# Moving weight units and activation buffers to other start addresses in SBUF, one core

## The reference

```python
# first block
proj  = rmsnorm(x, g_mix) @ w_in                  # 1024 -> 4804, attention inputs and gates
x     = x + merged_attention(proj, mem) @ w_out
hid   = square(relu(rmsnorm(x, g_mlp) @ w_mlp_in))  # 1024 -> 4096
x     = x + hid @ w_mlp_out
# second block: four of these (f = 0..3), with a gated mixer after f = 0
# and an attention after f = 2
def swiglu(x, w1, w3, w2):                        # 1024 -> 2816 -> 1024
    return (silu(x @ w1) * (x @ w3)) @ w2
h = layer_norm(ALPHA * h + 0.5 * swiglu(h, w1, w3, w2), g, b)
mix = (u * mixed) @ sgu_w_out                     # the gated mixer; u, v = split(gelu(h @ sgu_w_in))
```

## Time and profile before

| | |
|---|---|
| median of 3 runs | 1497.84 us (1495.8 to 1498.41) |
| the profiled execution's own time | 1496.87 us |
| its span, first to last instruction | 1495.1 us |
| TensorE busy | 1443.5 us, 97% of the span |
| VectorE busy | 930.3 us, 62% |
| ScalarE busy | 660.5 us, 44% |
| mean granted TensorE clock | 0.987 of full speed |
| HBM read | 261.92 MB, 178 GB/s over the span |

### The profile page before, as it was taken

The page is one execution under the profiler, slowest core; times in us unless marked ns, Lnnn a source line. Parts: engine busy times, 40 slices in busy tenths (PEclk is TensorE's granted clock), DMA queues, the critical chain, the costliest instruction groups (busy, mean ns, idle before and its releaser), DMA issues.

```text
span 1495.1 us, 25330 instructions
## 1 busy us (share of the span) xinstructions
PE 1443.5 (97%) x10484; PEld 1319.8 (88%) x10484; DVE 930.3 (62%) x1363; ACT 660.5 (44%) x834; POOL 95.7 (6%) x78
## 2 busy tenths in 40 slices
PE   8998998999999999999999999999999998999997
PEld 6987987899899999999789999999999886799996
DVE  5877457555675555657885555746555767665556
ACT  5655534333444434545244334425333467543342
POOL 0012141000020000100020000100000100100000
PEclk9999998999999999999999999999999999999999
DMA  7442444676577555655355555567555430465551
GB/s 256 151 141 88 153 142 155 218 222 215 189 235 272 193 186 188 198 193 197 113 186 201 186 191 197 192 202 253 188 184 193 157 135 24 141 205 191 195 196 57
DMA packets 191526, 268.43 MB, mean 180 GB/s; under 512 B 5740, under 2 KB 164752, under 8 KB 191182
## 3 DMA queue, kind: packets, MB, share of 16 engines
q1 hardware_dynamic: 186336, 250.05, 50.5%
q0 software_dynamic: 4224, 15.91, 3.1%
q10 hardware_dynamic: 878, 1.21, 0.3%
HBM read 261.92 MB, written 4.19 MB: 178 GB/s over the span
## 4 chain that ended last, share of the span: by engine, by line
PE 84%; DVE 9%; ACT 3%; DMA 2%; issue 1%; POOL 0%; DVEq 0%; ACTq 0%
PE bank L750 82%; DVE split L2009 2%; DMA ring<-in_ffn_w 2%; PE bank L773 1%; ACT split L1539 1%; DVE resid L2086 1%; DVE resid L2094 1%; DVE stats L2065 1%; DVE resid L2063 1%; ACT act_out L1561 0%; DVE arena L2601 0%; DVE stats L2023 0%; DVE arena L2206 0%; ACT gain_rows L1665 0%; DMA resid<-in_x 0%
## 5 line engine op out<-in xcount | busy, mean ns | idle before, releaser
L2009 DVE TENSOR_TENSOR split<-ring,split 128x2048 fp32r<-128x2048 f32 x212 | 484.4, 2286 | 371.2 <-ACT split L1539 365.8
L750 PE MATMUL bank<-hT_hi,split 128*128 128x256 f32 (+1 forms) x3984 | 699.9, 278 | 8.3 <-ACT act_out L1677 5.4
L750 PEld LDWEIGHTS bank<-hT_hi,split 128*128 128x128 f32 (+1 forms) x3984 | 609.2, 188 | 16.9 <-issue 9.8
L1539 ACT ACTIVATE split<-ring 128x2048 fp32r<-128x2048 f32 (+1 forms) x224 | 428.4, 1913 | 353.7 <-PE bank L750 318.2
L750 PE MATMUL bank<-hT_lo,split 128*128 128x256 f32 (+1 forms) x1992 | 552.4, 277 | 0.0
L750 PEld LDWEIGHTS bank<-hT_lo,split 128*128 128x128 f32 (+1 forms) x1992 | 375.3, 188 | 2.3
L750 PE MATMUL bank<-split,hid_hi 128*128 128x512 f32 x992 | 288.7, 397 | 0.0
L750 PEld LDWEIGHTS bank<-split,hid_hi 128*128 128x128 f32 x992 | 183.1, 189 | 39.1 <-issue 0.8
L750 PE MATMUL bank<-split,hT_hi 128*128 128x256 f32 (+1 forms) x896 | 178.0, 296 | 7.4 <-DVE split L2009 4.4
L750 PE MATMUL bank<-split,hid_lo 128*128 128x512 f32 x496 | 158.9, 393 | 0.0
L750 PEld LDWEIGHTS bank<-split,hT_hi 128*128 128x128 f32 x896 | 142.7, 189 | 15.8 <-issue 5.8
(11 more groups left out here) (216 smaller groups left out, 964.7 us busy)
## 6 DMA issues: line engine op xcount, KB each, us to landing
ring<-in_ffn_w SPq DMA_DIRECT2D x132, 1024.0 KB, 5.1
ring<-in_w_in SPq DMA_DIRECT2D x19, 1024.0 KB, 5.1
ring<-in_w_mlp_in SPq DMA_DIRECT2D x16, 1024.0 KB, 5.7
ring<-in_w_mlp_out SPq DMA_DIRECT2D x16, 1024.0 KB, 4.8
ring<-in_sgu_w_in SPq DMA_DIRECT2D x16, 1024.0 KB, 5.3
ring<-in_sgu_w_out SPq DMA_DIRECT2D x8, 1024.0 KB, 4.9
ring<-in_kv_w SPq DMA_DIRECT2D x6, 1024.0 KB, 5.2
ring<-in_w_out SPq DMA_DIRECT2D x4, 1024.0 KB, 5.0
```

The source lines that it names most:

```text
L750: ins = pe.matmul(o, lhsT, rhs, start=start, stop=stop)
L1539: act.activation(halves(q, n)[0], ring[:, u % SLOTS, 0:n], ACT.Copy).then_inc(hi_ready, 1)
L2009: dve.tensor_tensor(lo, ring[:, u % SLOTS, 0:n], hi.bitcast(F32), ALU.subtract).then_inc(split_ready, 1)
```

## The change

No instruction is added, removed or moved: each engine's list of instructions is the same before and after, row for row. Only start addresses differ. `LINE` becomes 512, so that a place is set modulo 512. The hi and lo halves of a `split` slot each get 128 spare elements, and a unit's start in its half depends on its kind.

Modulo 512 bytes the starts are now, with those of before in brackets:

- units that move token by token: 320 (192); the other units of the MLP, of FFNs 0 and 3, of the mixer, gates, `wout`, `q`, `wo`: 192 (192)
- units of the second FFN (f = 1) past its first chunk's `w1` and `w3`: 384 (192); units of the third (f = 2): 256 (192)
- `hid_hi`, `hid_lo`: 128 (320); `two`, `arena`: 128 (384); `const`: 128 (384); `hT_hi`, `hT_lo`, `ring`, `resid`, `xn`: 128 (128)

In the loops `halves` is asked for the unit one body later (`q + BODY`), since the first unit of the MLP's loop body moves token by token in its first turn and not in the later ones.

```diff
-LINE = 256
+LINE = 512
+SPARE = LINE // 4
+SHIFT = 32
...
+def by_token(name):
+
+    if name[0] in ("w1", "w3"):
+        return name[1] in TOK and name[2] == 0
+    return name[0] in ("proj", "sv") or name in (("mu", 0), ("mu", 1), ("kv", KV_ORDER[0]), ("kv", KV_ORDER[1]))
+
+
+def split_shift(q):
+
+    name = SPLIT_NAMES[q]
+    if by_token(name):
+        return SHIFT
+    if name[0] in ("w1", "w3", "w2"):
+        return {1: SHIFT + SHIFT // 2, 2: SHIFT // 2}.get(name[1], 0)
+    return 0
...
-        place(64)
+        place(128)
         with nc.sbuf_tensor("shared_rows", [P, 3 * MLP_BODY * 512], F32) as shared_rows:
...
         place(192)
-        split = sb("split", [P, SPLIT, 2, UNIT], F32R)
+        split = sb("split", [P, SPLIT, 2, UNIT + SPARE], F32R)
...
-            return [r[:, place, 0:n] for r in (split_hi, split_lo)]
+            at = split_shift(q)
+            return [split[:, place, part, at:at + n] for part in range(2)]
...
-                act.activation(halves(q, n)[0], ring[:, u % SLOTS, 0:n], ACT.Copy).then_inc(hi_ready, 1)
+                act.activation(halves(q if i is None else q + BODY, n)[0], ring[:, u % SLOTS, 0:n],
+                               ACT.Copy).then_inc(hi_ready, 1)
```

More of the change, by code:

```diff
@@ L208 @@
     n for n in plan_units() if n[0] != "cw")}
+SPLIT_NAMES = list(SPLITS)
 ORDER = plan_units()
@@ L380, in take @@
                                **{x: s for x, s in zip(names[:-1], shape[:-1])})
-        split_hi, split_lo = split[:, :, 0, :], split[:, :, 1, :]
         xn_flat = xn[:].rearrange("p b d -> p (b d)")
@@ L1072, in split_in_turn @@
                 pe.wait_ge(split_ready, i * BODY + (AHEAD + q + 1))
-                return [r.rearrange("p (k c) -> p k c", k=tiles) for r in halves(q, UNIT)]
+                return [r.rearrange("p (k c) -> p k c", k=tiles) for r in halves(q + BODY, UNIT)]
             def mlp(n):
@@ L2007, in low_unit @@
                 n = width(name)
-                hi, lo = halves(q, n)
+                hi, lo = halves(q if i is None else q + BODY, n)
                 dve.tensor_tensor(lo, ring[:, u % SLOTS, 0:n], hi.bitcast(F32), ALU.subtract).then_inc(split_ready, 1)
@@ L2660, in low_unit @@
             def low_unit(name):
-                q, u, place = SPLITS[name], UNITS[name], split_slot(SPLITS[name])
+                q, u = SPLITS[name], UNITS[name]
+                hi, lo = halves(q, UNIT)
                 pool.wait_ge(hi_ready, q + 1)
                 pool.wait_ge(split_ready, AHEAD + q)
-                pool.tensor_tensor(split_lo[:, place, :], ring[:, u % SLOTS, :], split_hi[:, place, :].bitcast(F32),
-                                   ALU.subtract).then_inc(split_ready, 1)
+                pool.tensor_tensor(lo, ring[:, u % SLOTS, :], hi.bitcast(F32), ALU.subtract).then_inc(split_ready, 1)
             pool.memset(zeros[:], 0.0)
```

## The result

The changed kernel takes 1507.41 us (median of 6, 1503.67 to 1511.03) against 1497.65 us; ratio 1.0065, 95% interval 1.0051 to 1.0079. The forecast was 1492.3, the range 1485 to 1503. The profiled execution took 1505.75 us.

The account below looks back on a forecast made before the run. TensorE's matmul pitch was taken to bound the kernel. Gains of 3.5 (tokens), 1.3, 0.6 and 0.3 (down units) less 0.2 (second memory unit) made 5.5 us, giving 1492.3 us; range 1485 to 1503.

Parts of the forecast that it names:

- What bounds the kernel: Whole kernel: TensorE, busy 97% of the span; outside seams, time is matmul count times pitch, so only pitch can move it.
- Features in FFNs 1 and 2: Feature matmuls with stationary starts 384 and 256 over moving 128: keep the fast 113.2 ns, nothing gained or lost.
- or 117.6: Upper bound in ns for the features of FFNs 1 and 2, the slow pitch already seen; would cost 8.9 us.
- rival 2: Features of FFNs 1 and 2 fall into the slow order, 8.9 us, time 1501.2; chance 0.22 with its wider form.
- Tokens: Token units at moving start 320 over stationary 128: 792 matmuls go from 117.6 to 113.2 ns, 3.5 us gained.
- Down units: Down matmuls: 1.3 us gained in MLP, mixer, FFNs 0 and 3; 0.6 in FFN 1; 0.3 in FFN 2.
- Features elsewhere: MLP, FFNs 0 and 3: own starts stay, only the down unit's hand-over may change; bounds nothing and 11.4 us, taken as nothing.
- The rule of the Trainium skill: TensorE has two independent SBUF read ports and never waits; taken to make the change worth nothing, the first rival, chance 0.26.

Follow-up runs that it names:

- experiment 5: Changed kernel with the starts of feature and down units set per FFN and MLP by a table in 64-byte steps; 1513.86 us, one run.
- experiment 7: experiment 1's kernel with hT, hid, two, arena and split all 64 bytes further; 1496.98 us, ratio 0.9985.
- experiment 9: Changed kernel with units of FFNs 1 and 2 moved by 256 bytes, to 448, in place of 192 and 64; 1497.58 us, ratio 0.9987.
- experiment 3: Kernel before, in the new split layout, with the token units alone moved by 128 bytes; 1498.29 us, ratio 1.0001.
- experiment 2: Kernel before, in the new split layout, with units of FFNs 1 and 2 alone moved, by 192 and 64 bytes; 1509.01 us, ratio 1.0070.
- experiment 4: Kernel before, in the new split layout, with hid, two, arena and const at 128 and no unit shifted; 1497.82 us, ratio 0.9988.
- experiment 11: experiment 1's kernel traced once more, unchanged; 1498.2 us, one run.
- experiment 12: The changed kernel traced once more, unchanged; 1507.6 us, one run.
- experiment 8: experiment 1's kernel with down units of the MLP and all four FFNs moving from 384; 1510.46 us, ratio 1.0080.
- experiment 1: Changed kernel with units of FFNs 1 and 2 put back to start 192, tokens at 320 and activations at 128 kept; 1496.39 us, ratio 0.9985.

## Why the prediction was wrong

**What bounds the kernel** was right: the 9 us are in the stages where TensorE hardly pauses, at a granted clock of 1.00, and there only pitches moved. The stage ahead of the MLP differs by up to 5 us between executions, with the change or without.

**The step that failed** is "Features in FFNs 1 and 2 ... I take 113.2: nothing", and with it the bound above it, "or 117.6". The two starts have pitches of their own, 119.9 and 118.6 to 118.7, above both pitches that the trace of before showed. They cost 6.2 and 5.0 us, 11.2 in all, where I had 0 with 8.9 as the worst. I had bounded an unseen pair of starts by the pitches of seen ones; experiments 5, 7 and 9 show that a pair is classed by its distance modulo 256, and no feature in the trace of before lay at the distances 0 and 128 of these two FFNs. This was rival 2, given 0.22, with the right place and too low a price.

**Tokens.** Right in kind and pitch (113.2). The mixer's gain is 1.5 us, and in all stages 2.5 (experiment 3) where I had 3.5; some short token stretches stay slow in each trace. 320 over 128 is distance 192, the features' own good one. What I had not seen is that features whose starts did not move are in the slow order behind them, in the mixer (+1.7) and `kv` (+0.8). Experiment 3 measured the whole of this step at 1.0001. In `kv` that goes with the tokens being fast, in all fourteen traces; in the mixer it came with the new layout even where the tokens stayed slow (experiments 2 and 4), so what it is owed to is not shown.

**Down units.** I took 231.2, 230.0 and 231.2 ns; the runs have 228.8, 227.9 and 232.3. The bounds, 229.0 to 233.3, held in the third and were just missed in the first; the second is lower still. The gain on TensorE is 3.6 ns x 1008 and 4.6 x 240, 4.7 us for my 1.9. But experiment 4, with all 62 units at 228.8 (5.4 us), came out at 0.9988, some 1.8 us. Its trace against that of before gives the reasons. The MLP and the four FFNs are 3.5 us shorter where their 55 down units alone would give 4.7: the features behind the faster units took 113.6 ns in place of 113.4, in the MLP 113.9 in place of 113.5, 0.9 us in all. And the features' slow order in the mixer and `kv` cost 2.5. FFNs that fall slow in some executions (about 4 us each, experiments 7, 11, 12) may come on top; how often they do was not measured.

**"Features elsewhere", taken as nothing,** is the second miss: mixer and `kv` lost 2.5 us of the 9. I had the mechanism, an order entered and then kept, and gave it a price only after down units. The sum of the first trace: 9.8 in FFNs 1 and 2 and 2.5 here, less 1.7 for tokens in the mixer and `kv` and 2.7 in the MLP and FFNs 0 and 3, is 8.0; the last 0.9 is the product's -0.7 and the queries' +1.7, which do not repeat.

**The rule of the Trainium skill** that I weighed against the trace (SBUF — State Buffer, "Who interferes with whom": TensorE's two read ports are independent and it never waits) does not hold here in the consequence that I drew from it, that a start address could not matter. The page itself says nothing of start addresses. With instructions, clock and other engines alike, a move of 192 bytes costs 6.5 ns on a 256-column matmul, and one of 256 bytes nothing. The runs show that the distance between the two streams matters; they do not show where in the memory or the engine the two meet.

## What to carry to other kernels

When a kernel is bound by back-to-back float32 matmuls, read the pitch of each kind of product from start to start, and tabulate it against the distance of moving from stationary start modulo 256; a map with another distance in each stage costs one run. An unseen distance must not be bounded by the pitches of seen ones. And judge a new distance in its sequence, since the stretch behind it may pay.

## What the runs showed of the hardware

- **Distance modulo 256.** By the moving operand's start less the stationary one's: features, 256 columns, take 113.4 to 113.9 ns at 192 (or 117.8, below), 117.7 or 117.8 at 64, 118.6 to 120.0 at 128, 119.8 to 120.0 at 0. Matmuls of 512 columns rank otherwise: 227.0 to 227.9 at 0, 228.8 to 229.8 at 64 (233.3 in single units and in `wout`, which had 228.9 in the first trace of the changed kernel and 233.4 in the second), 232.3 at 128, 232.7 to 233.7 at 192. Distances off the 64-byte grid, one run, gave 117.3 to 120.1, and 231.4 to 236.8 or, for three units, 226.7.
- **Two orders at one distance.** At distance 192 a stretch runs at 113.5 or 117.8 from its first matmuls to its last, over as many as 960 matmuls and the down units between (which are at 229.8 in place of 228.8 in such an FFN). At distance 64 tokens had the same two pitches, mostly 117.8, but 113.3 in the earlier trace rows and in `kv` of experiment 4. Which one it is goes with the product before. Features at 192 behind down units at distance 0 were always slow (experiment 8); at 128 fast in all steady chunks of five traces; at 64 mostly fast, slow in whole FFNs of experiments 7, 11 and 12. Directly behind fast tokens they were slow, 21 times of 21. The mixer's features were fast in both traces of the kernel before and slow in the twelve others, which share the new layout of `split`; whether that tells them apart stays open.
- **A version below both.** Tokens, features and down units at distances 192, 192 and 64 (experiment 1) measure 0.9985 [0.9972, 0.9998] of before, and its runs lie from 1490 to 1503 us. The spread of 12 us, against 7 in 29 runs of the kernel before on the same chip, fits FFNs that are fast or slow by execution; it is not shown to be that.
